# A two-block transformer kernel on one core: first product by row tile, weight splits ahead of the borders, attention turns lagging by three, four low halves on GpSimd

## The reference

```python
proj = x @ a_w_in            # index queries and keys, then k, v, then q
scores = sum_h w_h * relu(iq_h @ ik)     # causal, 512 x 512
picked = the 128 largest scores of each row   # rows 128..511 need a choice
p = softmax(q @ k over picked keys); o = p @ v
h = layer_norm(alpha * h + o @ a_w_o)
h = layer_norm(alpha * h + square(relu(h @ w_up)) @ w_down)
```

## Time and profile before

| | |
|---|---|
| median of three runs | 2002.26 us (2001.55 to 2005.41) |
| the profiled execution, its own time | 2006.59 us |
| its span on the core | 2004.8 us |
| mean granted clock of PE | 0.972 |
| PE, DVE, ACT, POOL busy | 94%, 60%, 37%, 6% of the span |

### The profile page before, as it was taken

The page is one execution under the profiler, slowest core; times in us unless marked ns, Lnnn a source line. Parts: engine busy times, 40 slices in busy tenths (PEclk is TensorE's granted clock), DMA queues, the critical chain, the costliest instruction groups (busy, mean ns, idle before and its releaser), DMA issues.

```text
span 2004.8 us, 23066 instructions
## 1 busy us (share of the span) xinstructions
PE 1890.7 (94%) x9192; PEld 1526.6 (76%) x9192; DVE 1196.7 (60%) x2201; ACT 734.5 (37%) x1142; POOL 115.2 (6%) x128
## 2 busy tenths in 40 slices
PE   7988899999999999999999999988899799999997
PEld 5764588888888888878788888767656688888886
DVE  3897758555555487467645455766776553333338
ACT  3526524222232443454332323255544452222221
POOL 0103200000000035000000000000031000000000
PEclk8999999999999999999999999899999899999999
DMA  5120224433433121132433333121000502323321
GB/s 176 64 71 14 76 72 160 156 126 126 167 127 106 65 84 43 64 126 64 155 118 121 110 118 119 59 79 50 22 1 1 178 22 90 120 93 96 105 84 43
DMA packets 116715, 184.06 MB, mean 92 GB/s; under 512 B 7120, under 2 KB 71632, under 8 KB 113536
## 3 DMA queue, kind: packets, MB, share of 16 engines
q1 hardware_dynamic: 115216, 177.77, 26.9%
q0 software_dynamic: 1392, 4.82, 0.9%
HBM read 180.47 MB, written 2.10 MB: 91 GB/s over the span
## 4 chain that ended last, share of the span: by engine, by line
PE 74%; DVE 17%; ACT 5%; issue 3%; POOL 0%; DMA 0%; DVEq 0%; SPq 0%; ACTq 0%
PE bank L590 10%; PE bank L592 10%; PE bank L591 10%; PE bank L768 6%; PE bank L769 6%; PE bank L767 6%; DVE wl L1808 3%; PE bank L564 2%; PE bank L566 2%; PE bank L565 2%; PE bank L825 2%; DVE gb L2176 2%; PE bank L809 1%; ACT wh L1199 1%; DVE m L2174 1%
## 5 line engine op out<-in xcount | busy, mean ns | idle before, releaser
L1808 DVE TENSOR_TENSOR wl<-raw,wh 128x2048 fp32r<-128x2048 f32 (+1 forms) x143 | 321.7, 2255 | 201.5 <-ACT wh L1199 201.2
L1199 ACT ACTIVATE wh<-raw 128x2048 fp32r<-128x2048 f32 (+1 forms) x143 | 267.2, 1885 | 237.1 <-PE bank L769 82.0
L590 PE MATMUL bank<-xh,wh 128*128 128x512 f32 (+2 forms) x880 | 348.1, 396 | 2.3 <-DVE wl L1808 2.3
L592 PE MATMUL bank<-xl,wh 128*128 128x512 f32 (+2 forms) x880 | 347.0, 394 | 0.0
L591 PE MATMUL bank<-xh,wl 128*128 128x512 f32 (+2 forms) x880 | 346.9, 394 | 0.0
L769 PE MATMUL bank<-wh,ul 128*128 128x512 f32 x592 | 230.4, 389 | 0.0
L768 PE MATMUL bank<-wl,uh 128*128 128x512 f32 x592 | 230.4, 389 | 0.0
L767 PE MATMUL bank<-wh,uh 128*128 128x512 f32 x592 | 230.4, 389 | 0.0
L590 PEld LDWEIGHTS bank<-xh,wh 128*128 128x128 f32 (+2 forms) x880 | 165.4, 188 | 42.2 <-DVE wl L1808 3.2
L592 PEld LDWEIGHTS bank<-xl,wh 128*128 128x128 f32 (+2 forms) x880 | 165.2, 188 | 38.9
L591 PEld LDWEIGHTS bank<-xh,wl 128*128 128x128 f32 (+2 forms) x880 | 165.4, 188 | 38.1
(11 more groups left out here) (355 smaller groups left out, 3104.6 us busy)
## 6 DMA issues: line engine op xcount, KB each, us to landing
raw<-in_mlp_w_up SPq DMA_DIRECT2D x32, 1024.0 KB, 5.6
raw<-in_mlp_w_down SPq DMA_DIRECT2D x32, 1024.0 KB, 5.0
raw<-in_w_ada SPq DMA_DIRECT2D x24, 1024.0 KB, 5.0
raw<-in_b_w_in SPq DMA_DIRECT2D x12, 1024.0 KB, 5.2
raw<-in_w_in SPq DMA_DIRECT2D x11, 1024.0 KB, 5.2
raw<-in_w_gate SPq DMA_DIRECT2D x11, 1024.0 KB, 5.3
raw<-in_w_up SPq DMA_DIRECT2D x11, 1024.0 KB, 5.4
raw<-in_w_down SPq DMA_DIRECT2D x10, 1024.0 KB, 5.0
```

What stands on the lines that cost most here:

```text
L590: pe.matmul(o, H[:, k, c], xh[:, k, :], start=k == 0, stop=False)
L592: step = pe.matmul(o, H[:, k, c], xl[:, k, :], start=False, stop=k == 7)
L1199: act.activation(slots[slot_of[i]][0][:, 0:n], raw[:, i % NRAW, 0:n], ACT.Copy).then_inc(*s_high.up(i))
L1808: dve.tensor_tensor(L[:, 0:n], raw[:, i % NRAW, 0:n], H[:, 0:n].bitcast(F), ALU.subtract).then_inc(*s_low.up(i))
```

## The change: what it does

1. Start: SP loads the identity alone (64 KB), x tile 0, chunk 0, x tiles 1 to 3, chunk 1; the rest of C goes to the small loads. PE transposes row tiles 0 and 1, then does the 12 matmuls of row tile 0, transposes tile 2, does row tile 1, and so on (`turn_alone`). ACT and DVE split x by row tile and half, chunk 0 behind tile 0 and chunk 1 behind tile 3.
2. Borders: `cur.take(..., n_groups + 1)` stands at the head of `cross` on ACT and DVE, and `reach` is gone.
3. Attention A: `LAG = {"A": 3, "B": 2}`, so the transposes come three turns behind the scores and `outs` four.
4. POOL makes the low halves of chunks 4, 5, 6 and 7: 4 and 5 ahead of its first rotary, 6 and 7 between its two. They signal on a semaphore of their own, `s_plow`.
5. In the plan of layer two's first panel, the w_ada chunk stands behind the second up-chunk and no longer between the two.

```diff
-                    elif q == 0:
+                    elif q == (1 if n == 0 else 0):
                         plan_ada(16 + n)
...
+        pool_low = (4, 5, 6, 7)
+
+        def low_of(i):
+            return (s_plow if i in pool_low else s_low).at(i)
...
+        small_loads.insert(0, (C[:, P:C_END], cst[:, P:C_END]))
...
+        LAG = {"A": 3, "B": 2}
...
-                    w.wait_ge(*s_low.at(i))
                     for t in range(T):
+                        if before and k0 == 0:
+                            before(t)
+                        w.wait_ge(*low_of(i))
...
-                            w.wait_ge(*s_xlow.at((x_key, kk)))
+                            w.wait_ge(*s_xlow.at(x_ready(t, kk) if x_ready else (x_key, kk)))
...
-                for u in range(N + 4):
+                lag = LAG[key]
+                for u in range(N + lag + 2):
                     if u < N:
                         scores(u)
-                    if 0 <= u - 2 < N:
-                        turn_p(2 * u - 4)
-                        turn_p(2 * u - 3)
-                    g = u - 3
+                    g = u - lag
+                    if 0 <= g < N:
+                        turn_p(2 * g)
+                        turn_p(2 * g + 1)
+                    g = u - lag - 1
                     if 0 <= g < N and g % 2:
                         outs(g // T, g % T // 2)
...
-            to_T("x", lambda t: h[:, t], lambda t: (s_h[t], 16 if t else 32))
+            def x_turned(t):
+                for u in ((0, 1), (2,), (3,), ())[t]:
+                    turn_alone("x", u, h[:, u], (s_h[u], 16 if u else 32))
+
             for i in range(2):
                 cur.make(skip)
-            gemm_tok("iq", 512, "x")
+            gemm_tok("iq", 512, "x", before=x_turned, x_ready=lambda t, k: ("x", t, k // 4))
...
             def cross(x_key, gain, shift, n_groups):
-                cur.take(high, 2)
+                cur.take(high, n_groups + 1)
                 cur.take(high, 0)
...
                 row(0)
                 row(1)
-                cur.reach(high, n_groups)
                 row(2)
...
             def low(i):
+                if i in pool_low:
+                    return
                 w.wait_ge(*landed(i))
...
             def cross(row_key, x_key, n_groups, evict):
-                cur.take(low, 2)
+                cur.take(low, n_groups + 1)
                 cur.take(low, 0)
...
-                    if t == 1:
-                        cur.reach(low, n_groups)
...
-            to_T("x")
-            for i in range(2):
-                cur.make(low)
+            for t in range(T):
+                for q in range(2):
+                    name, c = ("x", "alone", t, q), slice(t * P, (t + 1) * P)
+                    w.wait_ge(*s_xhigh.at(("x", t, q)))
+                    dve.tensor_tensor(xl[:, 4 * q:4 * q + 4, c], bank[banks.of.get(name, 0)][:, :].rearrange("p (k s) -> p k s", k=4),
+                                      xh[:, 4 * q:4 * q + 4, c].bitcast(F), ALU.subtract).then_inc(
+                                          *s_xlow.up(("x", t, q), *([("x", k) for k in range(4 * q, 4 * q + 4)] if t == T - 1 else [])))
+                    banks.read[name] = s_xlow.at(("x", t, q))
+                if t in (0, 3):
+                    cur.make(low)
...
+            def low(i):
+                n = chunks[i][1] * chunks[i][2]
+                H, L = slots[slot_of[i]]
+                w.wait_ge(*landed(i))
+                w.wait_ge(*s_high.at(i))
+                pool.tensor_tensor(L[:, 0:n], raw[:, i % NRAW, 0:n], H[:, 0:n].bitcast(F), ALU.subtract).then_inc(*s_plow.up(i))
+
+            low(4)
+            low(5)
             w.wait_ge(*s_act.at(("kv", T - 1)))
             w.wait_ge(*s_step.at("rot ik"))
             rotary("rot k", kd.rearrange("p t (g k) -> p t g k", k=64), 8)
+            low(6)
+            low(7)
...
-            sp.dma_start(C[:, :], cst).then_inc(s_h[0], 16)
+            sp.dma_start(ident, cst[:, C_ID:C_ID + P]).then_inc(s_h[0], 16)
             for t in range(T):
                 sp.dma_start(h[:, t, :], x[0, t * P:(t + 1) * P, :]).then_inc(s_h[t], 16)
-            fetch(0)
+                if t == 0:
+                    fetch(0)
```

More of the change, by code:

```diff
@@ L519, in parts @@
                 return H, L, nk, ncol
[L521 to L533, removed]
             def turn(key, src, nt, ready):
@@ L542, in turn, with gemm_tok @@
                     step.then_inc(*s_turn.up((key, j)))
-            def gemm_tok(key, n, x_key, ticks=0, last_ticks=None, after=None):
+            def gemm_tok(key, n, x_key, ticks=0, last_ticks=None, after=None, before=None, x_ready=None):
                 for t in range(T):
@@ L1199, in high @@
                 act.activation(slots[slot_of[i]][0][:, 0:n], raw[:, i % NRAW, 0:n], ACT.Copy).then_inc(*s_high.up(i))
-            def to_T(key, scale=None, shift=None, cols_ready=None):
-                for k in range(8):
-                    ps = bank[banks.of[key, k]][:, :]
-                    w.wait_ge(*s_turn.at((key, k)))
-                    if scale is None:
-                        act.activation(xh[:, k, :], ps, ACT.Copy).then_inc(*s_xhigh.up((key, k)))
-                    elif shift is None:
-                        act.activation(xh[:, k, :], ps, ACT.Copy, scale=scale[:, k:k + 1]).then_inc(*s_xhigh.up((key, k)))
-                    else:
-                        if k > 1:
-                            w.wait_ge(*s_xlow.at((key, k - 2)))
-                        if cols_ready:
-                            w.wait_ge(*s_step.at(cols_ready))
-                        act.activation(mid[k % 2], ps, ACT.Identity, bias=shift[:, k:k + 1],
-                                       scale=scale[:, k:k + 1]).then_inc(*s_act.up((key, "mid", k)))
-                        banks.read[key, k] = s_act.at((key, "mid", k))
-                        if k % 2 == 0:
-                            w.wait_ge(*s_act.at((key, "mid", k)))
-                            act.activation(xh[:, k, :], mid[k % 2], ACT.Copy).then_inc(*s_xhigh.up((key, k)))
             def turned_to(key, nt, dst):
@@ L1368, in attend @@
                                            accum_out=sm[:, hd, t:t + 1]).then_inc(*s_act.up((key, "exp", i)))
-                    g = u - 2
+                    g = u - lag
                     if 0 <= g < N:
@@ L1384, in attend @@
                     yield
-            to_T("x")
-            for i in range(2):
-                cur.make(high)
+            for t in range(T):
+                for q in range(2):
+                    name = ("x", "alone", t, q)
+                    w.wait_ge(*s_turn.at(name))
+                    act.activation(xh[:, 4 * q:4 * q + 4, t * P:(t + 1) * P], bank[banks.of.get(name, 0)][:, :].rearrange("p (k s) -> p k s", k=4),
+                                   ACT.Copy).then_inc(*s_xhigh.up(("x", t, q)))
+                if t in (0, 3):
+                    cur.make(high)
             w.wait_ge(*s_step.at("angle"))
```

43 lines of the change are left out of this document (12 added, 31 removed).

## The result

The changed kernel takes 1981.76 us (median of 4 executions, 1978.95 to 1984.04) against 2002.33 of the kernel before: ratio 0.9894, 95% interval 0.9875 to 0.9913. It is faster by 20.6 us; 28 were forecast, and 1981.76 lies inside the range of 1960 to 1987.

A forecast was written before the change was run, and what follows sets the result against it. The prediction took PE, busy 94% of the span, as the bound, leaving its gaps and the lowered clock behind them to win. 6 + 0 + 9 + 13 = 28 off 2006.59, less 4.3, gave 1974 us; range 1960 to 1987.

The forecast's parts named there:

- Start, 6: First product: PE starts it about 8.1 us earlier; gain taken as 6 us, bounds 4 to 8.5.
- Four low halves, 0: Choice of keys: POOL relieves DVE but holds it off twice, 2.5 + 4.2 − 3 x 2.2 = 0; bounds −9 to +1.
- PE stands some 8 us before chunk 8: Choice of keys: DVE still makes low half 8 late, at 131, so PE waits some 8 us for it.
- what is held off has two SBUF inputs: Choice of keys: POOL's subtraction and DVE's two-input SBUF instructions hold each other off for a whole instruction; MAX8 and MATCH_REPLACE8 aren't held.
- Lag three, −9: First attention: period falls from 10.2 to 9.1 us over eight periods, gain 9 us; bounds 0 to 12.
- I followed one period: First attention: one period traced by durations, PE 8.7 to 8.9, DVE 8.0 to 8.3 plus some 0.6 waiting; result 9.1 us.
- one short wait of PE for a copy: First attention: the only PE wait expected within the 9.1 us period.
- Borders, −13: Three borders: waits of 11.8 us go, the clock stays up; sum 13 us gained, bounds 8 and 16.
- I let it take back: Behind the third border: the moved w_ada step, now in DVE's dense stretch, was assumed to cost 1.3 us.
- From the sum to the median: Whole kernel: 28 us off the profiled 2006.59 gives 1978.6, then 4.3 less gives the median forecast, 1974.
- the median lies 4.3 below that execution: Whole kernel: offset of 4.3 us between the profiled execution and the median, subtracted from 1978.6 to reach 1974.

The follow-up runs named there:

- start_old: Changed kernel with the start's change undone (old transposes and splits of x ahead of the first product, old transfer order): 1984.69 us, ratio 0.9899.
- dve_all: Changed kernel with the four low halves moved from POOL back to VectorE (DVE): 1982.46 us, ratio 0.9885.
- pool5678: Changed kernel with low halves 5, 6, 7 and 8 on POOL and 4 on VectorE: 1982.12 us, ratio 0.9885.
- lag2: Changed kernel with lag two in place of three in the first attention: 1988.97 us, ratio 0.9919.
- copy_first: Changed kernel with VectorE copying its turned tile before its divisions in the first attention: 1974.53 us, ratio 0.9846.
- copies_first: As copy_first, with ScalarE also copying its turned tile before its exponentials: 1968.61 us, ratio 0.9817.
- borders_old: Changed kernel with the borders' low halves back in the middle of the border and the w_ada step moved back: 1993.37 us, ratio 0.9947.
- after_again: The changed kernel, unedited, timed once more beside other runs: 1981.4 us, ratio 0.988.

## Why the prediction was right, and where it was wrong

*Start, 6.* Right: the first matmul at 12.11 (11 to 12 said), the last copy at 38.31 (38 said), 6.0 ahead, of which start_old gives 5.0 back.

*Four low halves, 0.* Right in size and in its parts. POOL's subtraction takes 4.59 to 4.63 (4.8 taken); the rounds begin 2.1 late (2.5 said); the first comparison waits 4.08 (4.2 said); the sum is 0.0, and dve_all shows it. "PE stands some 8 us before chunk 8" was 9.2. The Trainium skill's figure (GPSIMD Engine Reference, § 3.1), by which the sum was −0.6, lies nearer to the 4.6 measured than mine did, though the sum itself came out at 0.0. But the rule, as I put it, that what is held off has two SBUF inputs, is too narrow: pool5678 shows a one-input TENSOR_SCALAR held for 4.3 us. The Trainium skill (SBUF — State Buffer, § Who interferes with whom) counts `tensor_scalar` in a two-port mode among what takes the lock; the prediction used only the other half of it. In the changed kernel this cost nothing, since low half 6 was caught by the comparison first.

*Lag three, −9.* The step that failed is "I followed one period", with "one short wait of PE for a copy": the period is 9.54 and not 9.1, because that wait is 1.17 us long. The gain was 5.9 by the stage in the trace, 5.2 by lag2's periods and 7.2 to 7.6 by its medians. What makes it long is order: both copies stood behind other work of their engines (copy_first, 8.95; copies_first, 8.25). PE's own work in a period is 9.54 − 1.17 = 8.4 and less, where the prediction had 8.7 to 8.9.

*Borders, −13.* The waits' 11.8 went, as borders_old shows from the other side, and the clock behind them is 1.00. By the trace the borders gave 15.7, since the 1.3 that "I let it take back" for the w_ada step was not taken back: the wait behind the third border is 0.60 and was 0.61.

*From the sum to the median.* This step cost most. The profiled executions stand 27.6 apart (2006.59 and 1978.95), and the sum said 28. The prediction then took 4.3 off, because "the median lies 4.3 below that execution". That was chance of one execution of the kernel before and no property of the next kernel, whose median lies 2.8 above its profiled execution. Over the five groups of runs the kernel before had medians from 2002.33 to 2005.91, and the changed kernel 1981.76 and 1981.4: 21 to 24 apart. The four kernels that undo a part lie 0.9 (dve_all), 7.4 (lag2), 11.8 (borders_old) and 3.1 (start_old) above 1981.6, the middle of its two medians, which makes 23.2 together. None of these four ran beside the changed kernel. If each is taken instead by its ratio to the kernel before that ran beside it, the four make 20. So the parts are worth 20 to 23. The other 4 to 7 of the 27.6 are chance of the two profiled executions: that of before lies 0.7 to 4.3 above the five medians of its kernel, that of after 2.6 below 1981.6. Falls of the clock that differ between executions, as after_again and lag2 show them, are of that size; that they alone make it up was not shown. The mean clock of an execution does not settle it: two of the changed kernel's four were both granted 0.978, and their spans are 1977.1 and 1981.9. Which of the parts is smaller than its stage in the trace (the start by 3, the borders by 4, if the medians are taken at their word) is not settled: the medians of one kernel, of four to nine executions each, lie up to 3.6 apart.

## What to carry to other kernels

Where a second engine takes work off the one that sets the end, go through every instruction of the first that can start under it, with one input or two, the engine's own pieces of the same work too; a wait that delays the helper by 0.9 us can be worth 4.3. Where a wait appears in the place of one removed, look at what the producer does ahead of the piece that is waited for, and check the engine that is named against its own timeline. And compare two kernels stage by stage at rows that both have, but size the whole by the medians of both, not by the offset of one profiled execution.

## What the runs showed of the hardware that I had not expected

- A TENSOR_SCALAR of 128x256 with one fp32 input in SBUF took 4.55 us in the place of 0.29 when it began 0.36 us behind a GpSimd subtraction of 128x2048 (pool5678). MAX8 and MATCH_REPLACE8 of 128x256 to 128x512 ran at 0.41 to 0.69 under the same subtraction.
- In stretches in which PE never stood, the granted clock fell to between 0.66 and 0.83 in a window of 10 us of the profile, and two executions of one kernel differ in it. In the first profile of the changed kernel such a fall lay at 430 us, and the second has, at the same place:

```profile
430.00:440.00 10.00, 10.00 (x62) 8.84 (x61) 4.20 (x6) 0.00 (x0) 0.00 (x0) 1.00 0.04 2
```

It shows 62 matmul instructions where the other had 49. By the granted clock such a fall costs 1.7 to 3.4 us of the 10; what sets it off there was not tested.
